# Moving the fourth tile's normed rows from VectorE to GpSimd and ScalarE in a two-layer decoder step

## What is computed

```python
def rmsnorm(x, g):
    y = xf * lax.rsqrt(jnp.mean(xf * xf, axis=-1, keepdims=True) + RMS_EPS)
    return (y * g.astype(jnp.float32)).astype(x.dtype)

# mixer
return x + mix @ w_out, ...
# experts
hf = rmsnorm(x, norm_g)
grp_logits, exp_logits = hf @ w_rg + b_rg, hf @ w_re + b_re     # router: which two experts
gates = ...                                                     # top 1 of 4 groups, top 2 inside it
y = sum_e ((silu(hf @ w_gate[e]) * (hf @ w_up[e]) * gates[e]) @ w_down[e])
return x + y
```

## Time and profile before

| | us |
|---|---|
| median of 3 runs | 810.37 (810.21 to 812.56) |
| the profiled execution, its own time | 810.1 |
| span of its trace | 808.3 |
| VectorE busy in the span | 601.0 (74%) |
| ScalarE busy | 478.4 (59%) |
| GpSimd busy | 331.7 (41%) |
| TensorE busy (matmuls, ends modelled) | 792.4 (98%) |

### The profile page before, as it was taken

The page is one execution under the profiler, slowest core; times in us unless marked ns, Lnnn a source line. Parts: engine busy times, 40 slices in busy tenths (PEclk is TensorE's granted clock), DMA queues, the critical chain, the costliest instruction groups (busy, mean ns, idle before and its releaser), DMA issues.

```text
span 808.3 us, 11933 instructions
## 1 busy us (share of the span) xinstructions
PE 792.4 (98%) x4092; PEld 628.5 (78%) x4092; DVE 601.0 (74%) x951; ACT 478.4 (59%) x816; POOL 331.7 (41%) x225
## 2 busy tenths in 40 slices
PE   9999999999999999999999999999999999999995
PEld 6887788878757888888588787888776678888861
DVE  5445655575789999999754456646658899999986
ACT  5633333612578888887663432444335798888874
POOL 0015996310042355664100199925012234656530
PEclk9999999999999999999999999999999999999998
DMA  8832223224959999998753322222379699999967
GB/s 295 288 117 66 78 66 118 105 79 150 409 187 386 375 362 377 398 370 296 273 187 104 86 73 71 66 80 91 99 296 346 240 416 347 387 377 396 342 226 287
DMA packets 57295, 188.17 MB, mean 233 GB/s; under 512 B 10862, under 2 KB 11886, under 8 KB 49036
## 3 DMA queue, kind: packets, MB, share of 16 engines
q1 hardware_dynamic: 44476, 156.56, 53.7%
q0 software_dynamic: 10368, 23.09, 7.7%
q10 hardware_dynamic: 2400, 7.87, 2.6%
HBM read 172.99 MB, written 29.39 MB: 250 GB/s over the span
## 4 chain that ended last, share of the span: by engine, by line
PE 55%; DVE 29%; issue 8%; DMA 6%; ACT 2%; DVEq 0%; SPq 0%; POOL 0%; ACTq 0%; POOLq 0%
PE ps L499 13%; PE ps L503 10%; PE ps L502 10%; DVE gul L2198 9%; DVE dnl L2203 7%; DVE hgTl L2214 4%; PE ps L501 3%; DMA back<-y_d 2%; PE ps L1483 2%; PE ps L1485 2%; PE ps L1484 2%; DVE y L2223 2%; DMA y_d<-y,rowidx 2%; PE ps L1462 2%; DVE act L2235 1%
## 5 line engine op out<-in xcount | busy, mean ns | idle before, releaser
L911 POOL DMA_INDIRECT y_d<-y,rowidx x32 | 118.2, 3695 | 121.6 <-DVE y L2223 114.5
L499 PE MATMUL ps<-wh,hT 128*128 128x512 f32 x408 | 163.5, 401 | 0.2
L2198 DVE TENSOR_TENSOR gul<-wgu,eh 128x1024 fp32r<-128x1024 f32 x128 | 150.7, 1222 | 0.1
L2189 DVE SCALAR_TENSOR_TENSOR wl<-raw,gcol,wh 128x512 fp32r<-128x512 f32 x80 | 78.5, 983 | 75.8 <-ACT wh L1133 75.7
L1164 ACT ACTIVATE eh<-wgu 128x1024 fp32r<-128x1024 f32 x128 | 128.5, 1057 | 4.0 <-PE ps L1485 3.9
L503 PE MATMUL ps<-wh,lT 128*128 128x512 f32 x313 | 122.4, 391 | 0.0
L502 PE MATMUL ps<-wl,hT 128*128 128x512 f32 x313 | 121.9, 390 | 0.0
L1483 PE MATMUL ps<-eh,hgTh 128*128 128x512 f32 x240 | 96.6, 402 | 0.4 <-issue 0.4
L1485 PE MATMUL ps<-eh,hgTl 128*128 128x512 f32 x240 | 93.8, 391 | 0.0
L1484 PE MATMUL ps<-gul,hgTh 128*128 128x512 f32 x240 | 93.5, 389 | 0.0
L1133 ACT ACTIVATE wh<-raw,gcol 128x512 fp32r<-128x512 f32 x80 | 57.3, 719 | 60.3 <-PE ps L501 56.2
(11 more groups left out here) (277 smaller groups left out, 1612.6 us busy)
## 6 DMA issues: line engine op xcount, KB each, us to landing
wgu<-in_gate_up SPq DMA_DIRECT2D x64, 1024.0 KB, 12.3
wdn<-in_w_down SPq DMA_DIRECT2D x64, 512.0 KB, 14.3
raw<-in_w_in SPq DMA_DIRECT2D x79, 256.0 KB, 2.7
raw<-in_w_out SPq DMA_DIRECT2D x32, 256.0 KB, 3.0
back<-y_d SPq DMA_DIRECT2D x16, 512.0 KB, 6.1
s<-in_state_ret POOLq DMA_DIRECT2D x8, 512.0 KB, 4.1
xn_d<-xf ACTq DMA_DIRECT2D x8, 512.0 KB, 7.6
x_in<-in_x_cols SPq DMA_DIRECT2D x8, 288.0 KB, 4.9
```

What stands on the lines that cost most here:

```text
L499: pe.matmul(out, both, w_h, start=first, stop=False)
L911: pool.indirect_dma_start(out=y_d, out_offset=bass.IndirectOffsetOnAxis(ap=rowidx[:, 1, e:e + 1], axis=0), in_=y[s][:, :], in_offset=None, ...
L2189: ve.scalar_tensor_tensor(out=wl[S % SPL][:, :], in0=raw[S % RAW][:, :], scalar=gcol[:, 0, L, s % KC:s % KC + 1], in1=wh[S % SPL][:, :].bi ...
L2198: ve.tensor_tensor(gu_pair(gul, gul3, e, s, p), gu_pair(wgu, wgu3, e, s, p), gu_split(e, p)[:, :].bitcast(F32), ALU.subtract).then_inc(glo, 1)
```

## The change

GpSimd now makes four products in each layer in place of two: for each half first tile 3's (128 rows), then the sample tile's (64 rows). ScalarE multiplies tile 3's product by rstd, in `scaled_rows(L, 3)`, which stands between the store of tile 2 and the copy of tile 3's transposes. VectorE's `xn_rows` for tile 3 is gone; its reciprocal for tile 3 now counts on `rstd_done`. On ScalarE the copy of tile 4's transposes and the second square sum of tile 4 change places. What follows from the counts is adjusted.

```diff
@@ GpSimd
                 for half in range(2):
                     cols = slice(512 * half, 512 * half + 512)
-                    pool.wait_ge(xw, 15 * L + NT * (1 + half) + NT)
-                    if half == 0:
-                        pool.wait_ge(sq_done, 16 * L + 2 * NT)
-                    else:
-                        pool.wait_ge(sq_done, 16 * L + 3 * NT + 1)
-                    pool.tensor_tensor(xn[1][LAST][0:NSAMP, cols], x[0:NSAMP, LAST, cols], gain[0:NSAMP, cols], ALU.mult).then_inc(xg_done, 1)
+                    for t in (3, LAST):
+                        n = tokens(t)
+                        pool.wait_ge(xw, 15 * L + NT * (1 + half) + t + 1)
+                        pool.wait_ge(sq_done, 16 * L + 2 * NT + (t + 2 if half else 0))
+                        pool.tensor_tensor(xn[1][t][0:n, cols], x[0:n, t, cols], gain[0:n, cols], ALU.mult).then_inc(xg_done, 1)
@@ ScalarE
-            def scaled_rows(L):
+            def scaled_rows(L, t):
 
-                sc.wait_ge(xg_done, 2 * (L + 1))
-                sc.wait_ge(rstd_done, 2 * L + 2)
-                sc.activation(xn[1][LAST][0:NSAMP, :], xn[1][LAST][0:NSAMP, :], ACT.Copy, scale=rstd[0:NSAMP, LAST:NT]).then_inc(xn_done, 1)
+                n = tokens(t)
+                sc.wait_ge(xg_done, 4 * L + t)
+                sc.wait_ge(rstd_done, 3 * L + t - 1)
+                sc.activation(xn[1][t][0:n, :], xn[1][t][0:n, :], ACT.Copy, scale=rstd[0:n, t:t + 1]).then_inc(xn_done, 1)
...
                     if t:
                         xn_out(L, t - 1)
+                    if t == 3:
+                        scaled_rows(L, 3)
                     ffn_rows(L, t)
                 xn_out(L, 3)
                 logits_out(L, 2)
+                ffn_rows(L, LAST)
                 ffn_square(L, LAST, 1)
-                ffn_rows(L, LAST)
                 logits_out(L, 3)
                 ffn_root(L, LAST)
 
-                scaled_rows(L)
+                scaled_rows(L, LAST)
@@ VectorE
                 last = ve.reciprocal(rstd[:, t:t + 1], rms[:, t:t + 1])
-                if t == LAST:
+                if t >= 3:
                     last.then_inc(rstd_done, 1)
-                    ve.wait_ge(rstd_done, 2 * L + 2)
+                    ve.wait_ge(rstd_done, 3 * L + t - 1)
...
                     ffn_scale(L, t)
-                    xn_rows(L, t)
+                    if t < 3:
+                        xn_rows(L, t)
                     x_add(ve, L, 2, t + 1)
                     ffn_rows(L, t)
```

More of the change, by code:

```diff
@@ L1142, in z_evac @@
                     if m == LAST or (m == 0 and g == 0):
-                        sc.wait_ge(rstd_done, 2 * L + 1)
+                        sc.wait_ge(rstd_done, 3 * L + 1)
                     func = ACT.Silu if g == 4 and t < LAST else ACT.Copy
@@ L2122, in mix_scale @@
                 ve.reciprocal(rstd[:, :], rms[:, :]).then_inc(rstd_done, 1)
-                ve.wait_ge(rstd_done, 2 * L + 1)
+                ve.wait_ge(rstd_done, 3 * L + 1)
             def ffn_rows(L, t):
```

## The result

The changed kernel takes 814.64 us (median of 7 runs, 813.23 to 815.4) where the kernel before takes 810.37. The ratio, taken over the executions of both and not from the two medians, is 1.0043 with a 95% interval of 1.0029 to 1.0058: 3.5 us slower. A repeat gave 1.0053 (1.0035 to 1.0070), 4.3 us. The forecast was 813.4 in a range of 811.2 to 814.5. The profiled execution took 813.23 us, the lowest of the seven, with a span of 811.4 against 808.3: +3.1, and the sum was +3.04.

What follows compares the result with a forecast made beforehand. A chain of waits over TensorE, then VectorE from 223.40, was taken to bound the kernel; +1.52 us a layer, +3.04 over two, on 810.1 gives 813.1, plus 0.27 for the median: 813.4, range 811.2 to 814.5.

Steps and rivals of the forecast that it cites:

- the sum: Per layer -0.41 + 0.85 + 1.08 = +1.52 us, counted for two layers: +3.04 us.
- The removed `xf`: Tile 3's `xf` gone from VectorE: tile 4's transposes start at 221.79 instead of 222.20, -0.41 us a layer.
- The added products: Two more GpSimd products of 128x512, 1.27 us each; their own time is hidden.
- The cover of 0.2 us: ScalarE's copy of tile 3's transposes, pushed to 222.0, still precedes TensorE's need at about 222.25.
- Place one: Tile 0's `xf` on VectorE, held by GpSimd's sample product; tile 1's transposes start later, +0.85 us a layer.
- Place two: First compare ranking the logits on VectorE, held by GpSimd's last product, +1.08 us a layer.
- Only place two: Rival: tile 0's `xf` goes first and only the compare is held; +1.3 us, 811.7; chance 0.14.
- only place one: Rival: the compare isn't held or the product comes after it; +0.9 us, 811.3; chance 0.08.
- neither: Rival: neither `xf` nor compare is held, leaving -0.41 us in each layer; 809.55; chance 0.08.
- More: Rival: place two's product itself held, or tile 3's late store delays the last; 0.5 to 1.5 us more; chance 0.08.
- The compare's sign: Expected trace sign: the first compare, 240 wide, at about 1.4 us instead of 0.41.
- first case: Both `xf` of tile 0 and the first compare are held: 813.4 us, running from 812.7 to 814.4; chance 0.62.

Runs made afterwards that it cites:

- Both repaired: Changed kernel, sample tile's first GpSimd product waiting for VectorE's tile 2 `xf`, tile 4's second square sum again ahead of its transposes' copy: ratio 0.9994, -0.5 us.
- Writes only: Changed kernel with each GpSimd product replaced by three memsets of the same half row: ratio 0.9989, -0.9 us against the kernel before.
- Alone: Kernel before, with only GpSimd's first-half sample product made to wait for tile 0's root, so it starts later: ratio 1.0019, +1.5 us.
- the run with the product behind the first compare: Kernel before, with ScalarE's transposes' copy ahead of tile 4's second square sum and a memset ahead of GpSimd's last product: ratio 1.0011, +0.9 us.

## Why the prediction was right, point by point

- **The removed `xf`, -0.41.** The transposes followed the last matmul by 2.00 us instead of 2.41, as worked out, with the idle matmul 0.22 us ahead of them. It was close: x was ready for the transposes at about 222.59 (the addition's end at 222.54 and 0.05 behind it, as before), 0.04 ahead of where the idle matmul let them start. "Both repaired" has this gain and 0.24 of a held compare, and its row numbers come 0.18 a layer earlier, for 0.17. "Writes only" measured 0.9 us for 0.82, but by luck: its row numbers come just 0.4 us earlier over both layers. The gap of 0.90 us on VectorE shows why 1.28 us of removed work gave a third of its length: the matmul was late next.
- **The added products.** 1.29 us for 128 rows against 1.27 for 64: the row of 512 elements counts. ScalarE's multiplication ran 221.18 to 222.33 and the copy behind it ended at 222.81, ahead of tile 4's transposes' second half. The cover of 0.2 us held, and both repairs together agree. It isn't more than that: 0.4 us more on GpSimd, in "writes only", were too much for it.
- **Place one, +0.85.** `xf` 2.28 us where 2.25 was forecast; the transposes waited 0.69, forecast 0.8. Tile 1's transposes start at 212.45 instead of 211.67, in an execution that stood 0.10 us earlier at that point (`xf` started at 209.51 and not 209.61): +0.88. Alone it measured 1.5 us for two layers, forecast 1.6, and 0.97 and 0.95 a layer up to the row numbers, so TensorE did carry it on.
- **Place two, +1.08.** The product started at T + 2.00 (forecast T + 2.0), the compare at T + 2.01 (2.05), and it ended at T + 3.53 (3.54). The lead of the product was 0.01 us and not the 0.05 forecast. That the compare was held and not the product is in part luck: the forecast named the order as open, and the margin is below what the starts on GpSimd can be trusted for. Had VectorE been clearly ahead, the run with the product behind the first compare shows how it goes, 0.44 us a layer.
- **The sum.** The gather's row numbers came at 232.30 in the first layer against 230.81; counted from tile 0's `xf`, which stood 0.10 earlier, that is +1.59, and +1.63 in the second layer, for +1.52. The span grew by 3.1 for 3.04. The profile agrees with the sum.
- **What was missing.** The median is 1.2 us above the forecast and 0.14 above the range's upper end; by the ratio (1.0043 times 810.37 = 813.85) it is 0.4 above the forecast and inside the range; the repeat's 4.3 us are 1.3 above the sum. The step that fell short is the sum's silence on TensorE: it took the chain of one layer through VectorE and added its holds, and put at nothing what TensorE does while it waits, which is to be idle longer and then to run for some microseconds at half its clock. I weighed the compare as a delay only. The runs put some 1.2 us on that, with the open interval given above. The first profile hardly shows it: its one fall, in the second layer, ended 4.8 us ahead of the gathered rows' transposes, and the time to them, 6.59 us, is that of the kernel before, 6.54. Why the median stands 1.4 us above the profiled execution stays open: the seven executions don't line up by their clocks (815.40 us at 0.997, 813.23 at 0.994).
- **The rivals.** "Only place two", "only place one" and "neither" are out by the rows of `xf` and the compare. "More" was to come from a product held at place two or from the late store: neither is in the trace, the last product took 1.26 us, and both repairs left no rest. What of it came true (814.64 lies in its range) did not come from what it named; of other causes the runs show the clock alone.
- **Slips in the working.** Three terms a layer, each up to 0.1 lower or 0.2 higher, make 0.6 down and 1.2 up over two layers: 812.8 to 814.6, and not 812.7 to 814.4, so the range ended inside its own first case. Nine tenths of 0.62 and the 0.08 of "more" are 0.64, not 0.62. Half to one and a half microseconds above 813.4 is 813.9 to 814.9, where "more" says 814.5 to 816. The compare's sign says 1.4 us where the working has 1.49. None of them moves the 813.4.

## What to carry to other kernels

Before elementwise work with SBUF inputs goes to GpSimd, draw its instructions on VectorE's timeline: in this kernel each VectorE instruction with two SBUF inputs that started under a product ended behind it, by nearly its own length, and moving a GpSimd instruction by a microsecond, or swapping two ScalarE instructions that release it, decides it. Copies, reductions and additions from PSUM kept their times beside such products here (the copy of the transposes 0.69 us, the reduction 0.40), so put the products under those and under gaps, or let them start behind the VectorE instruction that is on the chain. And when a chain's wait gets longer, look at what TensorE's clock does behind it, in more than one execution: the delay itself is not all of the price.

## What the runs showed of the hardware

- With starts nearly equal (224.63 on GpSimd, 224.64 on VectorE; 0.00 to 0.02 apart in all twelve layers that show this hold) it was GpSimd that went first, and the VectorE instruction then showed as running for 1.52 us, not as waiting. One that started 0.12 us ahead kept its 0.41. Between them nothing was measured. The profile's times on GpSimd are rough, so whether the lead decided, or something else at a near tie, isn't shown.
- At place one the pair of products ended at 210.71, so the second began at about 209.44 (1.27 us each), 0.07 us ahead of `xf`; that too was enough.
- A compare whose two inputs are the same tensor, `duel<-lg`, is held like one with two tensors. In the prediction it was left as a bound.
- The memsets that took the products' place held neither: 1.29 and 0.41 us.
- A wait of TensorE that is 1.1 us longer, 1.8 and then 0.3 to 0.9 us, was followed by a granted clock of 0.50 for 3.4 to 7 us in six of eight layers, and matmul pairs of 1.0 us took up to 2.06. With five idle matmuls put into the wait there was none in four layers.
